# A GLA/attention/MoE decoder on one core: all three parts of the output gate are projected before the head outputs, by step 19

## The chip, the cores and the metric

The kernel runs on one core of a Trainium2 chip. A core has five engines that each work through a queue of instructions of their own and wait for one another by semaphores: TensorE (PE in the profile; its weight loads are PEld), VectorE (DVE), ScalarE (ACT), GpSimd (POOL) and SyncE (SP, which here only issues DMAs). The metric is the device time in microseconds of one execution. Three runs of the kernel before took 1502.73, 1507.63 and 1510.17 us, median 1507.63.

## The reference

Two layers, each a token mixer, a cross-attention into a fixed memory and a mixture of experts, over 512 tokens of width 1024, all in fp32. The change lies in the mixer:

```
h = rms_norm(x, norm_mix[l])
z = h @ w_in[l]          # one projection, split into
(g_q, g_k, g_v, g_lr, g_r, d_q, d_k, d_v, i_q, i_k, i_w, c_u) = split(z)
log_a = log_sigmoid(g_lr @ gla_wa2 + gla_ba) / 16
o_gla = gla_chunked(g_q, g_k, g_v, log_a)        # 4 heads of 48 x 96, with a decaying state
o_gla = rms_norm(o_gla, gla_onorm) * silu(g_r)   # g_r: the output gates, 384 wide
o_dsa = dsa_attention(...)                       # 6 heads, each query keeps its top 128 keys
o_conv = conformer_conv(c_u, ...)                # GLU, 31 causal taps, layer norm, silu
x = x + concat(o_gla, o_dsa, o_conv) @ w_out[l]
x = x + memory_cross_attention(...)
x = x + hierarchical_moe(...)                    # 16 experts, top 1 group, top 2 experts
```

## The kernel before

Each layer has a mixer block, a cross-attention block and an expert block. In the mixer block the columns of w_in come in nine chunks, and each chunk is projected in jobs (the list JOBS): one job fills one bank of PSUM (ps0 and ps1 in turn) by eight pieces, one for each 128 rows of w_in. A job may begin only when ScalarE has copied out the job before the last (the semaphore proj_out). Behind the first jobs (indexer, queries, keys, values) come 24 attention steps: six heads for each of four tiles of 128 queries. Step n handles head n % 6 of tile n // 6, and the width of its work grows with the tile from 128 to 512 keys.

In step n TensorE issues, in this order: the turning of the exponentials of step n by matmuls with a diagonal of inverse sums (L850, "turn n", into the one bank ps6); in even steps the logits of steps n+2 and n+3 (L841) and the values of steps n-2 and n-1 (L862); then the filling work of that step. The filling work is the jobs that attention doesn't need: ca, cg (convolution), gq, gk, gv (the gated linear attention, GLA), kt (keys turned, L742), upd (state parts, three jobs, L750), gr (output gates, three jobs gr0, gr1, gr2 of 128 gate columns each, L728) and o (the outputs of the four GLA heads, L763 and L765). One product of the seven levels of the GLA's decay (L790) goes into each of steps 12 to 18, after the first two pieces of filling. In step 22 comes the sum for the convolution's mean (L899), which needs all taps.

ScalarE in step n: the exponential of step n+1 (L1040); then the copies out of PSUM of all jobs whose last piece stood in step n-1 (L958, for the states L951, for head outputs L939 and behind each but the first a square, L943); only then the copy of turn n out of ps6 (L1059), for which turn n+1 on TensorE waits. VectorE masks (L1205), takes inverses of sums (L1210), merges the level products (L1255), and does the convolution's 62 taps (L1222) spread over steps 5 to 21. GpSimd adds biases, makes the inverse diagonals (L1365), and in the step before STATES clears the buffer of the states (L1390), for which it waits for kt. SyncE loads parts of w_out once the last gv job is done (L664) and once the last o job is done (L666, L667), then mem (L669).

Which job's pieces stand in which step is worked out when the program is built. Each kind of piece has a cost in LENGTH, attention(n) a cost for each step, and for three phases of steps (0 to 3, 4 to 8, 9 to LAST_FILLED - 1) the cost of the phase's jobs and steps divided by the number of steps is its pace. A step takes pieces from the list until its sum reaches the pace; o jobs may not come before step FIRST_O. Steps in which a job ends set other work: STATES (where VectorE adds up the states) is the step after that in which the last upd ends, and the taps are spread by VectorE's estimated load around it. The lines are:

```
LENGTH = dict(ca=0.7, cg=0.7, gq=0.87, gk=0.87, gr=0.87, gv=0.65, kt=0.6, upd=0.7, o=1.5)
GATES, GATED, LAST_FILLED, FIRST_O = 4, 9, 23, 20
```

Of the kernel before, what the change touches and what calls it, by code (L numbers as in the profile page):

```python
# [24 lines left out]
P = 128  # L25
# [3 lines left out]
GH, GK, GV, RANK = 4, 48, 96, 16  # L29
# [99 lines left out]
def program(nc, A, out):  # L129
    ctx = ExitStack()  # L130
    with ctx:
# [8 lines left out]
        def view(t, off, *shape, rows=P):  # L140
            n = int(np.prod(shape))
            ap = t[0:rows, off:off + n]
            names = "abcd"[:len(shape)]
            if len(shape) > 1:
                ap = ap.rearrange(f"p ({' '.join(names)}) -> p {' '.join(names)}",
                                  **{names[i]: shape[i] for i in range(1, len(shape))})
            return ap
# [266 lines left out]
        for l in range(L):  # L414
# [14 lines left out]
            gv = view(arena, up + 3072, NT, GH * GV)  # L429
            gr = view(arena, up + 4608, GC, S)  # L430
# [57 lines left out]
            JOBS = [(0, 0, ID + RANK + IH, "T", "ik", 0)]  # L488
# [6 lines left out]
            JOBS += [(7, 0, GH * GV, "tok", "gv", i) for i in range(NT)]  # L495
            JOBS += [(None, 0, P, "kt", "kt", i) for i in range(2)]
            JOBS += [(8, 0, P, "T", "gr", 0)] + [(None, 0, P, "upd", "upd", c) for c in range(3)]
            JOBS += [(8, P, P, "T", "gr", 1)] + [(None, 0, GV, "o", "o", h) for h in range(2)]
            JOBS += [(8, 2 * P, P, "T", "gr", 2)] + [(None, 0, GV, "o", "o", h) for h in range(2, GH)]
            NJ = len(JOBS)  # L500

            def k_of(chunk):
# [6 lines left out]
            def done(name):  # L509
# [6 lines left out]
                        kt=lambda i: kdecT[:, :, i, :])  # L516
            AFTER_IDX = done("iq")
            STEPS = [(i, h) for i in range(NT) for h in range(AH)]
            NS = len(STEPS)
# [5 lines left out]


            LENGTH = dict(ca=0.7, cg=0.7, gq=0.87, gk=0.87, gr=0.87, gv=0.65, kt=0.6, upd=0.7, o=1.5)
            GATES, GATED, LAST_FILLED, FIRST_O = 4, 9, 23, 20

            def attention(n):  # L530

                i, h = STEPS[n]
                return 0.3 * (i + 1) + (0.9 if 11 <= n < NLEV + 13 else 0.0)

            def filler(names, steps):

                return sum(LENGTH[JOBS[n][4]] for n, c in parts if JOBS[n][4] in names) + sum(attention(n) for n in steps)

            parts, pace = [], 0.0
            for n in range(BEFORE_STEPS, NJ):  # L540
                for c in range(KD if JOBS[n][0] is not None else 1):
                    parts.append((n, c))
            phases = ((("ca", "cg"), range(GATES)), (("gq", "gk"), range(GATES, GATED)),
                      (("gv", "kt", "gr", "upd", "o"), range(GATED, LAST_FILLED)))
            paces = [filler(names, steps) / len(steps) for names, steps in phases]
            work_of, left, spent = [], list(parts), 0.0
            for n in range(NS):
                pace += paces[(n >= GATES) + (n >= GATED)]
                spent += attention(n)
                mine = []  # L550
                while left and (spent < pace or n == NS - 1) and not (JOBS[left[0][0]][4] == "o" and n < FIRST_O):
                    mine.append(left.pop(0))
                    spent += LENGTH[JOBS[mine[-1][0]][4]]
                work_of.append(mine)
# [1892 lines left out]
```

How the kernel before makes its waits and increments, by code:

```python
            def do(ins, mark=None, wait=True):  # L243
                s = sN[mark] if mark else own
                count[s] = count.get(s, 0) + 1
                ins.then_inc(s, 1)
                if wait:
                    eng.wait_ge(s, count[s])
# [6 lines left out]
        def inverse_roots(act, do, banks, n, summed, mark, rows=P, outs=None):  # L255
            for m, bank in enumerate(banks):
                act.wait_ge(sN[summed], m + 1)
                do(nc.scalar.activation(ps[bank][0:rows, :], ps[bank][0:rows, :], ACT.Ln, bias=epst[0:rows, :], scale=1.0 / n))
            for m, bank in enumerate(banks):
                out = outs[m][0:rows, :] if outs else ps[bank][0:rows, :]
                do(nc.scalar.activation(out, ps[bank][0:rows, :], ACT.Exp, scale=-0.5), mark, wait=False)
# [101 lines left out]
        def add_rows(dve, l, k, t):  # L364
            xt = x[:, t, :]
            if k == LAST:
                dve.wait_ge(sN["hot_out"], t + 1)
                dve.wait_ge(s_add, summed(l, HIGH, t))
                rows, g = psw[:, 512 * LAST_BANK(t):512 * LAST_BANK(t) + D], gates[:, t, 1:2]
            else:
                dve.wait_ge(s_yg[NT * k + t], 16 * (l + 1))
                if k == HIGH:
                    dve.wait_ge(s_add, summed(l, LOW, t))
                rows, g = ya[k][t], early[:, t:t + 1] if k == HIGH else gates[:, t, 0:1]
            nc.vector.scalar_tensor_tensor(xt, rows, g, xt, ALU.mult, ALU.add).then_inc(s_add, 1)
```

## Time and profile before

| | |
|---|---|
| runs | 1502.73, 1507.63, 1510.17 us, median 1507.63 |
| profiled execution | 1509.55 us, span 1507.7 us, mean granted TensorE clock 0.979 |
| TensorE busy | 1431.0 us, 95% |
| VectorE busy | 1152.7 us, 76% |
| ScalarE busy | 887.7 us, 59% |
| GpSimd busy | 595.7 us, 40% |
| chain that ended last | PE 46%, DVE 25%, DMA 15%, issue 7%, ACT 5% |
| HBM | 287.76 MB read, 29.50 MB written, 210 GB/s over the span |

Busy time is what an engine computes, without waits. The chain that ended last is followed back from the last instruction, at each step to what released it, and says by engine where the end was decided. The attention steps of layer 0 run from about 127 to 284 us, those of layer 1 from about 870 to 1028 us. In a row of the timeline stand the start and the length in us, the engine, the line, the operation, what it writes and reads, how many instructions were merged, and in square brackets the idle time before the first of them and what ended it. The length of the last matmul is printed up to its modelled end, so the next group can start a little before it is over. One matmul in the program is one or more instructions in the trace (a 512-wide fp32 product is two).

### The profile page before, as it was taken

Reading aid. Unit: us, or ns where it says so; the run is one execution under the profiler, and the core shown is the slowest. Engines: PE = TensorE matmul, PEld = TensorE weight load, DVE = VectorE, ACT = ScalarE, POOL = GpSimd, SP = SyncE. Lnnn points to the kernel's source line nnn. Section 1 sums busy time; section 2 is a strip of 40 time slices with the busy share of each in tenths; the row PEclk is TensorE's granted clock in tenths of the full one; section 3 lists DMA queues with packets and bytes.
Section 4 is the critical chain, followed back from the end, with each engine's and each line's share of the span. In section 5 each row is a group of like instructions: output and inputs, shape, how many; then the busy total and the mean of one; then the engine's idle time right before and its main releaser. Section 6 shows DMA issues by size and latency. Waiting matters only on the chain.

```text
span 1507.7 us, 20546 instructions
## 1 busy us (share of the span) xinstructions
PE 1431.0 (95%) x6830; PEld 1052.0 (70%) x6830; DVE 1152.7 (76%) x1658; ACT 887.7 (59%) x1300; POOL 595.7 (40%) x288
## 2 busy tenths in 40 slices
PE   7999999999999999999799999999989899999995
PEld 4678566567577888877556865665766788887773
DVE  5696887334489999999757958873335899999996
ACT  5733344643558878888485522348345488887880
POOL 2333364060005665554542425521400066655544
PEclk9999999999999999999899999999998899999998
DMA  6333601312149999999651421105041599999995
GB/s 228 95 84 70 222 10 47 140 59 98 70 162 340 399 399 399 398 399 399 216 185 42 112 81 71 57 1 198 1 167 42 183 362 398 398 398 398 398 388 181
DMA packets 151485, 312.75 MB, mean 207 GB/s; under 512 B 33158, under 2 KB 46380, under 8 KB 151228
## 3 DMA queue, kind: packets, MB, share of 16 engines
q1 hardware_dynamic: 140300, 271.39, 49.8%
q0 software_dynamic: 6624, 24.12, 4.3%
q10 hardware_dynamic: 4496, 16.40, 2.7%
q8 instruction: 37, 0.61, 0.2%
q14 instruction: 28, 0.23, 0.0%
HBM read 287.76 MB, written 29.50 MB: 210 GB/s over the span
## 4 chain that ended last, share of the span: by engine, by line
PE 46%; DVE 25%; DMA 15%; issue 7%; ACT 5%; POOL 1%; DVEq 1%; POOLq 0%; SPq 0%; ACTq 0%
PE ps L710 13%; DMA arena<-in_w_down 11%; DVE rest_w_down L1436 8%; PE ps L728 7%; PE ps L1518 4%; DVE rest_w_up L1436 4%; PE ps L1540 3%; DVE rest_w_gate L1436 2%; DVE xg_rest L1449 2%; PE ps L817 2%; PE ps L1636 2%; ACT head_w_down L1431 2%; PE ps L731 2%; DMA arena<-in_w_gate 1%; PE ps L850 1%
## 5 line engine op out<-in xcount | busy, mean ns | idle before, releaser
L2112 POOL TENSOR_TENSOR rest_w_down<-arena,head_w_down 128x2048 fp32r<-128x2048 f32 x30 | 193.4, 6448 | 189.4 <-ACT head_w_down L1431 189.4
L1436 DVE TENSOR_TENSOR rest_w_down<-arena,head_w_down 128x2048 fp32r<-128x2048 f32 x30 | 153.5, 5116 | 12.0 <-ACT head_w_down L1431 11.9
L1436 DVE TENSOR_TENSOR rest_w_gate<-arena,head_w_gate 128x2048 fp32r<-128x2048 f32 x64 | 145.8, 2279 | 0.1
L1436 DVE TENSOR_TENSOR rest_w_up<-arena,head_w_up 128x2048 fp32r<-128x2048 f32 x64 | 143.5, 2281 | 0.1
L1431 ACT ACTIVATE head_w_down<-arena 128x2048 fp32r<-128x2048 f32 x60 | 115.2, 1926 | 39.1 <-DMA arena<-in_w_down 38.9
L1431 ACT ACTIVATE head_w_gate<-arena 128x2048 fp32r<-128x2048 f32 x60 | 114.4, 1919 | 36.1 <-DMA arena<-in_w_gate 35.5
L1431 ACT ACTIVATE head_w_up<-arena 128x2048 fp32r<-128x2048 f32 x64 | 122.0, 1940 | 10.5 <-DMA arena<-in_w_up 10.4
L1420 PE MATMUL ps<-head_w_gate,xg_head 128*128 128x512 f32 x256 | 104.8, 409 | 2.5 <-DVE xg_rest L1449 1.9
L728 PE MATMUL ps<-hT,arena 128*128 128x512 f32 x224 | 104.3, 602 | 2.6 <-ACT arena L951 2.6
L1410 PE MATMUL ps<-head_w_down,he_head 128*128 128x512 f32 x240 | 99.2, 413 | 5.8 <-DVE rest_w_down L1436 2.9
L1422 PE MATMUL ps<-head_w_gate,xg_rest 128*128 128x512 f32 x256 | 101.0, 395 | 0.0
L1421 PE MATMUL ps<-rest_w_gate,xg_head 128*128 128x512 f32 x256 | 101.0, 395 | 0.0
L1420 PE MATMUL ps<-head_w_up,xg_head 128*128 128x512 f32 x256 | 99.8, 390 | 0.0
L1422 PE MATMUL ps<-head_w_up,xg_rest 128*128 128x512 f32 x256 | 99.7, 390 | 0.0
L1421 PE MATMUL ps<-rest_w_up,xg_head 128*128 128x512 f32 x256 | 99.6, 389 | 0.0
L1222 DVE SCALAR_TENSOR_TENSOR mixr<-arena,cf,mixr 128x512 f32<-128x512 f32 x120 | 94.8, 790 | 3.2
L2059 POOL DMA_INDIRECT xg<-hrows,slot_tok x2 | 4.9, 2437 | 229.5 <-DVE slot_tok L2030 229.5
L1411 PE MATMUL ps<-rest_w_down,he_head 128*128 128x512 f32 x240 | 93.9, 391 | 0.0
L1412 PE MATMUL ps<-head_w_down,he_rest 128*128 128x512 f32 x240 | 93.9, 391 | 0.0
L710 PE MATMUL ps<-hT_head,w_rest 128*128 128x512 f32 x224 | 89.8, 401 | 0.0
L2105 POOL DMA_INDIRECT xg<-hrows,idx x28 | 76.4, 2727 | 21.0 <-POOL idx L2118 21.0
L1443 ACT ACTIVATE xg_head<-ps,cf 128x128 fp32r<-128x128 f32 x256 | 69.2, 378 | 25.2 <-PE ps L1712 15.8
(381 smaller groups left out, 3519.2 us busy)
## 6 DMA issues: line engine op xcount, KB each, us to landing
arena<-in_w_gate SPq DMA_DIRECT2D x64, 1024.0 KB, 9.9
arena<-in_w_up SPq DMA_DIRECT2D x64, 1024.0 KB, 11.5
arena<-in_w_down SPq DMA_DIRECT2D x64, 1024.0 KB, 10.7
arena<-in_w_in SPq DMA_DIRECT2D x10, 1536.0 KB, 6.7
yrows<-yb ACTq DMA_DIRECT2D x30, 512.0 KB, 6.2
arena<-in_w_in SPq DMA_DIRECT2D x4, 2048.0 KB, 8.7
x<-in_x SPq DMA_DIRECT2D x8, 512.0 KB, 13.9
arena<-in_w_in SPq DMA_DIRECT2D x16, 256.0 KB, 4.9
```

What stands on the lines that cost most here:

```text
L710: last = nc.tensor.matmul(o, lhs, rhs, start=(c == 0 and a == 0), stop=(c == KD - 1 and a == 2))
L728: last = nc.tensor.matmul(ps[n % 2][0:width, :], w[:, c, col:col + width], hT[:, c, :], start=(c == 0), stop=(c == KD - 1))
L1222: do(nc.vector.scalar_tensor_tensor(o, cin[:, i, j:j + S], convw[:, i, j:j + 1], o, ALU.mult, ALU.add))
L1410: nc.tensor.matmul(out, ah, bh, start=(c == 0), stop=False)
L1411: nc.tensor.matmul(out, ah, bl, start=False, stop=False)
L1412: last = nc.tensor.matmul(out, al, bh, start=False, stop=(c == n - 1))
L1420: nc.tensor.matmul(ps[q][:, :], xh[:, c, :], wh[q][:, c, :], start=(c == 0), stop=False)
L1421: nc.tensor.matmul(ps[q][:, :], xh[:, c, :], wl[q][:, c, :], start=False, stop=False)
L1422: last = nc.tensor.matmul(ps[q][:, :], xl[:, c, :], wh[q][:, c, :], start=False, stop=(c == KD - 1))
L1431: nc.scalar.activation(wh[q][:, part(q, j), :], raw[q][:, part(q, j), :], ACT.Copy).then_inc(s_head[q], 1)
L1436: nc.vector.tensor_tensor(wl[q][:, c, :], raw[q][:, c, :], wh[q][:, c, :].bitcast(F32), ALU.subtract).then_inc(s_split[q], 1)
L2112: nc.gpsimd.tensor_tensor(wl[2][:, c, :], raw[2][:, c, :], wh[2][:, c, :].bitcast(F32), ALU.subtract)\
```

## The change

The list of jobs now has gr1 and gr2 together, ahead of all four head outputs. Phase three is paced over steps 9 to 19 and counts no o jobs. The head outputs have a first step each: 20 for o0 and o1, 22 for o2 and o3.

```
--- before.py
+++ after.py
@@ -495,8 +495,7 @@
             JOBS += [(7, 0, GH * GV, "tok", "gv", i) for i in range(NT)]
             JOBS += [(None, 0, P, "kt", "kt", i) for i in range(2)]
             JOBS += [(8, 0, P, "T", "gr", 0)] + [(None, 0, P, "upd", "upd", c) for c in range(3)]
-            JOBS += [(8, P, P, "T", "gr", 1)] + [(None, 0, GV, "o", "o", h) for h in range(2)]
-            JOBS += [(8, 2 * P, P, "T", "gr", 2)] + [(None, 0, GV, "o", "o", h) for h in range(2, GH)]
+            JOBS += [(8, P * i, P, "T", "gr", i) for i in (1, 2)] + [(None, 0, GV, "o", "o", h) for h in range(GH)]
             NJ = len(JOBS)
 
             def k_of(chunk):
@@ -525,7 +524,7 @@
 
 
             LENGTH = dict(ca=0.7, cg=0.7, gq=0.87, gk=0.87, gr=0.87, gv=0.65, kt=0.6, upd=0.7, o=1.5)
-            GATES, GATED, LAST_FILLED, FIRST_O = 4, 9, 23, 20
+            GATES, GATED, LAST_FILLED, FIRST_O = 4, 9, 20, (20, 20, 22, 22)
 
             def attention(n):
 
@@ -541,14 +540,14 @@
                 for c in range(KD if JOBS[n][0] is not None else 1):
                     parts.append((n, c))
             phases = ((("ca", "cg"), range(GATES)), (("gq", "gk"), range(GATES, GATED)),
-                      (("gv", "kt", "gr", "upd", "o"), range(GATED, LAST_FILLED)))
+                      (("gv", "kt", "gr", "upd"), range(GATED, LAST_FILLED)))
             paces = [filler(names, steps) / len(steps) for names, steps in phases]
             work_of, left, spent = [], list(parts), 0.0
             for n in range(NS):
                 pace += paces[(n >= GATES) + (n >= GATED)]
                 spent += attention(n)
                 mine = []
-                while left and (spent < pace or n == NS - 1) and not (JOBS[left[0][0]][4] == "o" and n < FIRST_O):
+                while left and (spent < pace or n == NS - 1) and not (JOBS[left[0][0]][4] == "o" and n < FIRST_O[JOBS[left[0][0]][5]]):
                     mine.append(left.pop(0))
                     spent += LENGTH[JOBS[mine[-1][0]][4]]
                 work_of.append(mine)
```

By the planner's own figures the pace of phase three goes from 5.16 to 5.70 a step. Where the pieces of filling stand:

| step | before | now |
|---|---|---|
| 10 | gv1 x7 | gv1 x8 |
| 11 | gv1, gv2 x4 | gv2 x7 |
| 12 | gv2 x4, gv3 | gv2, gv3 x5 |
| 13 | gv3 x6 | gv3 x3, kt0, kt1, gr0 |
| 14 | gv3, kt0, kt1, gr0 x2 | gr0 x4 |
| 15 | gr0 x3 | gr0 x3, upd0, upd1 |
| 16 | gr0 x3, upd0 | upd2, gr1 x4 |
| 17 | upd1, upd2, gr1 x3 | gr1 x4 |
| 18 | gr1 x3 | gr2 x4 |
| 19 | gr1 x2 | gr2 x4 |
| 20 | o0, o1, gr2 x3 | o0, o1 |
| 21 | gr2 x4 | none |
| 22 | gr2, o2, o3 | o2, o3 |

STATES goes from step 18 to 17, and with it GpSimd's clearing from step 17 to 16. Of VectorE's taps, step 17 has 0 instead of 3 and step 18 has 6 instead of 3; the others stay.

The order of TensorE's instructions, first from the values of step 16 on (L862 values, L728 gr, L790 level product, L750 upd, L850 turn). Before:

```order
L862 MATMUL ps<-scratch 64x128 x6
L728 MATMUL ps<-hT,arena 128x512 x2
L790 MATMUL ps<-mixg 128x64 x16
L728 MATMUL ps<-hT,arena 128x512
L750 MATMUL ps<-arena 128x192 x2
L850 MATMUL ps<-arena,scratch 128x128 x3
L750 MATMUL ps<-arena 128x192 x4
L790 MATMUL ps<-mixg 128x64 x16
L728 MATMUL ps<-hT,arena 128x512 x3
```

Now, from turn 15 on; a line number of this kernel is one less than before (L727 gr, L789 level product, L749 upd, L849 turn, L840 logits, L861 values):

```order
L849 MATMUL ps<-arena,scratch 128x128 x3
L727 MATMUL ps<-hT,arena 128x512 x2
L789 MATMUL ps<-rs 128x64 x16
L727 MATMUL ps<-hT,arena 128x512
L749 MATMUL ps<-arena 128x192 x4
L849 MATMUL ps<-arena,scratch 128x128 x3
L840 MATMUL ps<-scratch 128x512 x2
L861 MATMUL ps<-scratch 64x128 x6
L749 MATMUL ps<-arena 128x192 x2
L727 MATMUL ps<-hT,arena 128x512
```

Before, upd1 and upd2 (the x4) are followed by a level product and then by gr1's first pieces; now upd0 and upd1 (the x4) close step 15, and turn 16, its logits and values and upd2 stand before gr1.

The second place is the end of step 20 up to step 22, from the last products of o1. Before:

```order
L763 MATMUL ps<-arena 96x128
L765 MATMUL ps<-arena 96x128
L728 MATMUL ps<-hT,arena 128x512 x3
L850 MATMUL ps<-arena,scratch 128x128 x4
L728 MATMUL ps<-hT,arena 128x512 x4
L850 MATMUL ps<-arena,scratch 128x128 x4
L862 MATMUL ps<-scratch 64x128 x8
L728 MATMUL ps<-hT,arena 128x512
L763 MATMUL ps<-arena 96x128 x2
```

Now, from the same products:

```order
L764 MATMUL ps<-arena 96x128
L762 MATMUL ps<-arena 96x128
L764 MATMUL ps<-arena 96x128
L849 MATMUL ps<-arena,scratch 128x128 x8
L861 MATMUL ps<-scratch 64x128 x8
L762 MATMUL ps<-arena 96x128 x2
```

The seven pieces of gr2 between o1 and turn 22 are gone, and turn 21 and turn 22 are printed as one group of eight.

## Rows read from the trace of the kernel before

**Rows 1.** Busy time by window, the attention steps of layer 0 and of layer 1.
```profile
core 0: us, PE busy (x) PEld busy (x) DVE busy (x) ACT busy (x) POOL busy (x), PEclk, DMA share, GB/s
126.80:284.00 157.20, 152.52 (x876) 100.40 (x875) 113.98 (x203) 60.54 (x137) 60.31 (x60) 0.99 0.24 85
870.40:1027.60 157.20, 152.54 (x876) 100.43 (x875) 114.02 (x203) 60.53 (x137) 60.00 (x60) 0.99 0.16 58
```

**Rows 2.** Waits of TensorE (line waiting, what it waited for: us, times, longest), 150 to 284 us.
```profile
PE ps L728 <- ACT arena L951: 1.3, 1, 1.3
PE ps L862 <- ACT scratch L1059: 0.9, 1, 0.9
PE ps L790 <- ACT arena L1051: 0.2, 1, 0.2
PE ps L742 <- ACT arena L958: 0.2, 1, 0.2
```

**Rows 3.** Timeline of TensorE, steps 16 to 18 (start, us, engine, line).
```profile
233.39 0.83 PE L850 MATMUL ps<-arena,scratch 128*128 128x128 f32 x6
...
236.02 1.98 PE L728 MATMUL ps<-hT,arena 128*128 128x512 f32 x4
...
242.15 1.47 PE L750 MATMUL ps<-arena 128*128 128x192 f32 x8
...
246.85 2.84 PE L728 MATMUL ps<-hT,arena 128*128 128x512 f32 x6 [1.30 <-ACT arena L951]
```

**Rows 4.** Timeline of TensorE, steps 20 to 22.
```profile
260.11 1.05 PE L850 MATMUL ps<-arena,scratch 128*128 128x128 f32 x8
...
266.32 2.74 PE L728 MATMUL ps<-hT,arena 128*128 128x512 f32 x6
268.89 1.05 PE L850 MATMUL ps<-arena,scratch 128*128 128x128 f32 x8
269.78 3.60 PE L728 MATMUL ps<-hT,arena 128*128 128x512 f32 x8
...
279.25 1.88 PE L899 MATMUL ps<-mixr,ones 128*128 128x512 f32 x4
```

**Rows 5.** Timeline of ScalarE, around step 21.
```profile
264.55 0.72 ACT L1040 ACTIVATE scratch<-scratch,small 128x512 f32<-128x512 f32 x1 [0.61 <-DVE small L1205]
...
266.52 1.79 ACT L939 ACTIVATE mixg<-ps 32x512 f32<-32x512 f32 x3 [0.68 <-PE ps L765]
268.33 0.63 ACT L943 ACTIVATE rs<-mixg 128x512 f32<-128x512 f32 x1
269.98 0.60 ACT L1059 ACTIVATE scratch<-ps 128x512 f32<-128x512 f32 x1 [1.02 <-PE ps L850]
```

**Rows 6.** Page, costliest groups: the convolution taps.
```profile
L1222 DVE SCALAR_TENSOR_TENSOR mixr<-arena,cf,mixr 128x512 f32<-128x512 f32 x120 | 94.8, 790 | 3.2
```

**Rows 7.** Timeline of VectorE: behind the last tap of layer 0.
```profile
269.36 0.06 DVE L1308 MEMSET small<- 128x1 f32 x1
```

**Rows 8.** Timeline of TensorE: the first matmuls behind four gaps.
```profile
128.87 0.49 PE L850 MATMUL ps<-arena,scratch 128*128 128x128 f32 x2 [2.04 <-POOL arena L1365]
...
373.91 2.34 PE L1606 MATMUL ps<-arena 64*128 64x256 f32 x14 [2.49 <-DVE arena L1895]
...
1117.55 1.78 PE L1606 MATMUL ps<-arena 64*128 64x256 f32 x14 [2.49 <-DVE arena L1895]
...
1479.12 0.47 PE L2177 MATMUL ps<-head_w_gate,he_head 128*128 128x512 f32 x1 [2.11 <-DVE he_rest L2321]
```

**Rows 9.** Busy time and granted clock (PEclk) by window, behind those gaps.
```profile
129.20:132.60 3.40, 3.40 (x12) 2.61 (x11) 3.23 (x10) 0.77 (x3) 1.21 (x3) 0.51 0.70 263
375.00:378.40 3.40, 3.40 (x14) 2.31 (x11) 2.79 (x4) 1.78 (x8) 0.00 (x0) 0.50 1.06 393
1117.60:1121.00 3.40, 3.40 (x23) 2.78 (x24) 2.13 (x3) 0.73 (x3) 0.00 (x0) 1.00 1.05 387
1479.20:1482.60 3.40, 3.40 (x15) 2.81 (x16) 0.81 (x1) 0.00 (x0) 0.71 (x1) 1.00 0.38 154
```

More of the change, by code:

```diff
@@ L497, in program @@
             JOBS += [(8, 0, P, "T", "gr", 0)] + [(None, 0, P, "upd", "upd", c) for c in range(3)]
-            JOBS += [(8, P, P, "T", "gr", 1)] + [(None, 0, GV, "o", "o", h) for h in range(2)]
-            JOBS += [(8, 2 * P, P, "T", "gr", 2)] + [(None, 0, GV, "o", "o", h) for h in range(2, GH)]
+            JOBS += [(8, P * i, P, "T", "gr", i) for i in (1, 2)] + [(None, 0, GV, "o", "o", h) for h in range(GH)]
             NJ = len(JOBS)
@@ L527, in program @@
             LENGTH = dict(ca=0.7, cg=0.7, gq=0.87, gk=0.87, gr=0.87, gv=0.65, kt=0.6, upd=0.7, o=1.5)
-            GATES, GATED, LAST_FILLED, FIRST_O = 4, 9, 23, 20
+            GATES, GATED, LAST_FILLED, FIRST_O = 4, 9, 20, (20, 20, 22, 22)
             def attention(n):
@@ L543, in program @@
             phases = ((("ca", "cg"), range(GATES)), (("gq", "gk"), range(GATES, GATED)),
-                      (("gv", "kt", "gr", "upd", "o"), range(GATED, LAST_FILLED)))
+                      (("gv", "kt", "gr", "upd"), range(GATED, LAST_FILLED)))
             paces = [filler(names, steps) / len(steps) for names, steps in phases]
@@ L550, in program @@
                 mine = []
-                while left and (spent < pace or n == NS - 1) and not (JOBS[left[0][0]][4] == "o" and n < FIRST_O):
+                while left and (spent < pace or n == NS - 1) and not (JOBS[left[0][0]][4] == "o" and n < FIRST_O[JOBS[left[0][0]][5]]):
                     mine.append(left.pop(0))
```

## The prediction

> **What bounds the kernel now.** The page comes first. TensorE is busy 95% of the span, and in the chain that ended last it has the largest share, so the first question is whether it ever stands still where the change works. The change is inside the 24 attention steps of each layer. The busy times by window show this stretch twice: 152.52 us of TensorE work in 157.20 us in layer 0, 152.54 in the same length in layer 1 [rows 1]. The two layers are the same here to 0.02 us, so I work out layer 0 and double it. Next come the waits of TensorE in the steps of layer 0 that carry projections of the gate and later chunks: 1.3 us for the states' copies, 0.9 us at the very end, 0.2 us twice [rows 2]. That is 2.6 us. All other engines have idle time in this stretch that nobody waits for. TensorE's work is therefore the bound, the change keeps that work (the same instructions in another order), and no order can save more than 2.6 us a layer. What it can do is make new idle time on TensorE. So the sum is one of waits, not of work.
>
> **The change part by part.** *What is moved.* The third part of gr (gr2, eight pieces of two matmuls) is now projected in steps 18 and 19, not in 20 to 22. By the row of eight matmuls that take 3.44 us to the next start (269.78, printed as 3.60 with its tail), a piece costs 0.86 us, eight 6.9 us [rows 4]. gv, kt, upd and gr1 move forward to make room. The jobs are only reordered: 0 us of work on TensorE. Turn 20, at 260.11 before, comes up to 6.9 us later, and everything behind it has 6.9 us less to do.
>
> *The states' wait that goes.* Before, upd0 stood in step 16 and upd1 and upd2 in step 17. They run from 242.15, one level product follows, and gr1's first piece starts only at 246.85, having idled 1.30 us until ScalarE had copied the state parts [rows 3]. It waits for the copy of upd1, which ScalarE takes up only behind the exponential of step 18. In the new order upd0 and upd1 close step 15, and turn, logits, values and upd2 of step 16 lie between upd1 and the first piece of gr1. Turn, logits and values of step 16 run from 233.39 to 236.02, 2.6 us, and one upd is half of the 1.47 us printed for two [rows 3]: 3.3 us in all, against the copies of gr0, upd0 and upd1, which at 0.60 us or a little over (a 512-wide copy, [rows 5]) are 2 us. I take the whole 1.30 us: -1.3.
>
> *Waits it adds before step 20.* upd1 now stands behind gr0's last piece with only upd0 between, and needs gr0's copy out of its bank. The copy takes 0.60 us and upd0 0.7 us of issue; with the matmul's tail (0.16 us between printed length and next start in most of [rows 4]) and two semaphores some 0.2 us are left: +0.2. Bounds are 0 and 0.8, the latter if ScalarE has just begun an exponential of 0.72 us [rows 5]. kt0 and kt1 now stand together; before, a level product of 2 us stood between them and 0.19 us of wait were left [rows 2]. Now kt1 waits for gv3's copy with only kt0, three transposes, as its cover: +0.2, with the same bounds for the same reason. GpSimd clears the states' buffer one step earlier and waits for kt1 there; what stands behind it on GpSimd is the bias of step 17 and the inverse of step 15, and the cleared buffer is needed some 10 us later: 0. Three convolution taps of 0.79 us [rows 6] move from step 17 to 18; all taps end at 269.36 [rows 7] and their mean is formed at 279.25 [rows 4], ten us later: 0. SyncE's loads of w_out and mem hang on the last head output, which moves by the sum below and no more.
>
> *The wait it makes in step 21.* This is the largest term. After head outputs o0 and o1 TensorE does turn 21, and turn 22 must wait until ScalarE has copied the result of turn 21 out of the one bank they share. ScalarE has queued, ahead of that copy, the three copies of o1 and a square. Before: o1's issue ends at 266.32, its copies run 266.52 to 268.31, the square to 268.96, and the copy of turn 21 comes at 269.98 [rows 4, 5]. TensorE never noticed, since three pieces of gr2 stood between o1 and turn 21 and four between turn 21 and turn 22. With no gr2 left, call the end of o1's issue E. Turn 21 runs E to E+0.89. ScalarE is free at E+2.64 (268.96 less 266.32), copies for 0.60, and turn 22 starts at E+3.28. TensorE idles 3.28 less 0.89: +2.4. Bounds: 2.0, if the square overlaps more than shown, and 3.2, if the exponential of step 22 is late and pushes o0's copy into o1's. VectorE and GpSimd are not later than this: once turn 20 is over, the mask of step 22, its exponential (0.72), three taps (0.79 each) and the inverse follow within an estimated 6 us by these lengths, and turn 22 stands more than 9 us behind turn 20.
>
> *Behind it.* Turn 22, values, o2, o3, the mean's product and turn 23 follow as before; the 0.9 us at the end (values 22, behind o3's copies) stays, as does the 0.2 us of the last level product [rows 2]: 0.
>
> Sum of waits: -1.3 +0.2 +0.2 +2.4 = +1.5 us a layer, +3.0 in all. By the bounds it is -1.3 +2.0 = +0.7 to -1.3 +0.8 +0.8 +3.2 = +3.5 a layer.
>
> *The clock.* TensorE idled 2.0 to 2.5 us at one go in six places of the span. Four stand in [rows 8]: 2.04 us before 128.87, 2.49 before 373.91 and again before 1117.55, 2.11 before 1479.12. In the 3.4 us just behind them (from 375.00 in the second case, where the level changed) the granted clock was 0.51, 0.50, 1.00 and 1.00 [rows 9]. The other two repeat the first, one at the same place of layer 1 and one before the last expert block of layer 0, with most of the stretch at half. So it is 1.2 GHz in four of six cases, 2.4 GHz in two. The new wait of 2.4 us is of this size, and none of the old ones in these steps is. What follows it is TensorE work without cover, so 3.4 us at half rate cost 1.7 us. With four in six it falls in one layer or in both: +1.7 or +3.4.
>
> The Trainium skill bears on this: "TensorE: Matmul & The Clock Gate", section "Why this matters for your kernels", says that throughput holds as long as no idle gap between bursts of matmuls is longer than one that is somewhat above this wait. By that rule the clock would stay up and the sum be +3.0. Four of the six rows just named speak against it and two for it, so it has its own case below.
>
> The sum is made against the profiled execution: span 1507.7, 1509.55 us with what lies around it. That is 1.9 us above the median of the runs shown, 1507.63, and inside their spread. Forecast: waits +3.0 and one fall of the clock +1.7, together +4.7, from 1507.63: 1512.3 us.
>
> **The rivals.**
> *The clock stays up.* The gaps of layer 1 before 1117.55 and 1479.12 show it can [rows 8, 9]. Then +3.0: 1510.6. (It is what the page of the Trainium skill named above would give.)
> *It falls in both layers.* Four of six gaps speak for it. Then +6.4: 1514.0.
> *Slower beyond doubt: a longer stretch at 1.2 GHz.* One mechanism, in step 21 of both layers: the wait behind o1's copies comes out near its upper bound 3.2 us (+0.8 a layer) and the clock stays down until the second wait, 0.9 us at values 22 some 9 us later, that is for about twice 3.4 us, costing 3.4 us a layer. Then 2 x (1.5 + 0.8 + 3.4) = +11.4: 1519.0. It decides from where the idle time in step 21 exceeds those six gaps. For it: the two waits lie close together. Against it: 0.9 us is far below the gaps that cost the clock.
> *Faster: the new wait is covered.* If the copy of turn 21 gets in before o1's last copies, or TensorE's own order leaves work between the two turns, only -1.3 +0.4 stay: -0.9 a layer, -1.8: 1505.8. Against it: ScalarE runs its queue in order, and before it, too, the copies of o1 came ahead of that of turn 21 [rows 5].
> *The change does not do what it says.* A planner sets the steps; the instruction order shows the third part of gr done before turn 20 and nothing of it after, so only the price can be nought: if the new wait merely replaces the old one, 1507.6. The lower bound +0.7 a layer is near it.
> *VectorE becomes the bound.* From the mask of step 19 it has 23 taps, 18 us [rows 6], and four masks and inverses, some 22 us together, and may start only after turn 17, near 248. It would end near 270, when TensorE is at turn 21. Ten us of room speak against it; I give it no time of its own.
>
> **How the numbers follow.** What a measurement of this kernel can tell from no change is about 0.5%, 7.5 us. Chances: one fall 0.35, clock up 0.22, both falls 0.22, longer low stretch 0.09, waits merely exchanged 0.07, faster 0.05. The first three all lie at +3 to +6.4, within 0.5%; with the spread of the medians (the three runs differ by 7.4 us) a third of the both-falls case and a tenth of the one-fall case may read as slower, which with the long stretch gives 0.20. Of the faster case a half would read as such: 0.03. Same 0.77. The range runs from the faster case, 1505, to just short of the long stretch, 1518.
>
> **What would show it.** Right: on TensorE in step 21 of both layers an idle gap of 2.4 us before the matmuls of turn 22, ended by ScalarE's copy of turn 21; the 1.3 us before gr1 gone; small waits at upd1 and kt1; the granted clock near 0.5 just behind the gap in one layer or both; the end of the steps 1.5 us later per layer plus 1.7 per fall. Wrong: turn 22 starting right behind turn 21; the steps shorter than before; or the end of the taps later than the last head output.

## The result

The changed kernel took 1512.55 us (median of nine runs, 1510.38 to 1516.24), the kernel before 1507.63 us beside it. One of the nine executions of the kernel before took 4994.01 us and is not in the ratio; the other eight have a median of 1506.82. The ratio is 1.0038, 95% interval 1.0024 to 1.0052: some 0.4% or 5.7 us slower. The interval leaves out 1, and the size is inside the 0.5% that the prediction called no change. In a second set of runs on another occasion it was 1.0048 (1.0034 to 1.0062).

The waits of TensorE in the attention steps of layer 0, in the columns of [rows 2]; all lines of the changed kernel are one lower than before:

```profile
PE ps L849 <- ACT scratch L1058: 2.4, 1, 2.4
PE ps L861 <- ACT scratch L1058: 0.9, 1, 0.9
PE ps L741 <- ACT arena L957: 0.4, 1, 0.4
PE ps L789 <- ACT arena L1050: 0.3, 1, 0.3
```

The 1.3 us behind the states' copies are gone and 2.4 us for ScalarE's copy of a turn (L1058) are new. The 0.9 us at the end are the same, the wait at the turned keys is 0.4 instead of 0.2 (L741), and the one at the last level product, 0.3 instead of 0.2 in this print, is 0.25 us in the timelines of both kernels. The timeline of TensorE shows where, with the same place of layer 1 last; it answers [rows 3, 4]:

```profile
219.16 0.55 PE L741 MATMUL ps<-cf,arena 128*128 128x128 f32 x3 [0.41 <-ACT arena L957]
...
234.02 1.77 PE L749 MATMUL ps<-arena 128*128 128x192 f32 x8
...
239.01 1.02 PE L727 MATMUL ps<-hT,arena 128*128 128x512 f32 x2
...
264.95 1.13 PE L840 MATMUL ps<-scratch 64*128 64x512 f32 x4
...
270.17 1.06 PE L849 MATMUL ps<-arena,scratch 128*128 128x128 f32 x8
...
273.58 1.44 PE L849 MATMUL ps<-arena,scratch 128*128 128x128 f32 x8 [2.36 <-ACT scratch L1058]
...
276.86 1.06 PE L762 MATMUL ps<-arena 128*96 128x128 f32 x4
...
280.37 1.88 PE L898 MATMUL ps<-mixr,ones 128*128 128x512 f32 x4
...
284.04 1.09 PE L861 MATMUL ps<-scratch 128*64 128x128 f32 x16 [0.90 <-ACT scratch L1058]
...
1021.29 1.61 PE L849 MATMUL ps<-arena,scratch 128*128 128x128 f32 x8 [2.36 <-ACT scratch L1058]
```

Turn 21 starts at 270.17, right behind o1, and turn 22 only at 273.58, having idled 2.36 us; in layer 1 the same. Turn 22 is printed with 1.44 us where turn 21 has 1.06 with the same work. ScalarE at that place, answering [rows 5]:

```profile
268.84 0.59 ACT L938 ACTIVATE mixg<-ps 96x512 f32<-96x512 f32 x1 [0.35 <-PE ps L764]
270.37 1.79 ACT L938 ACTIVATE mixg<-ps 32x512 f32<-32x512 f32 x3 [0.94 <-PE ps L764]
272.19 0.63 ACT L942 ACTIVATE rs<-mixg 128x512 f32<-128x512 f32 x1
272.84 0.60 ACT L1058 ACTIVATE scratch<-ps 128x512 f32<-128x512 f32 x1
273.34 0.72 ACT L1039 ACTIVATE scratch<-scratch,small 128x512 f32<-128x512 f32 x1
```

o0's copy, three copies of o1, the square, the copy of turn 21, the exponential, one behind another. The square ends at 272.82, 2.65 us after 270.17 where o1's issue ends; 2.64 was worked out. The copy of turn 21 ends at 273.44, and turn 22 starts 0.14 us later. The busy times by window, the first two from turn 6 (the first one 256 keys wide) to the first head-sum product behind the steps, (L909 now, L910 before) in layers 0 and 1, then in each layer the 3.4 us that begin 0.7 and 0.5 us after the start of turn 22:

```profile
core 0: us, PE busy (x) PEld busy (x) DVE busy (x) ACT busy (x) POOL busy (x), PEclk, DMA share, GB/s
166.24:285.07 118.83, 114.87 (x720) 74.14 (x718) 86.84 (x136) 48.47 (x107) 49.12 (x44) 0.99 0.17 58
913.98:1032.77 118.79, 114.86 (x719) 74.13 (x717) 86.86 (x136) 48.46 (x107) 48.82 (x44) 0.99 0.08 28
274.30:277.70 3.40, 3.40 (x24) 2.85 (x23) 0.10 (x1) 0.60 (x1) 0.60 (x1) 0.50 0.02 5
1021.80:1025.20 3.40, 3.40 (x24) 2.85 (x23) 0.16 (x1) 0.35 (x2) 0.60 (x1) 0.50 0.00 0
```

The same two stretches of the kernel before:

```profile
core 0: us, PE busy (x) PEld busy (x) DVE busy (x) ACT busy (x) POOL busy (x), PEclk, DMA share, GB/s
168.60:283.94 115.34, 112.70 (x720) 72.92 (x718) 86.49 (x136) 48.62 (x107) 49.00 (x44) 1.00 0.17 60
912.24:1027.56 115.32, 112.69 (x719) 72.92 (x717) 86.52 (x136) 48.61 (x107) 48.69 (x44) 1.00 0.08 29
```

The stretch is 118.83 instead of 115.34 us, 3.5 us longer in each layer, and the granted clock is 0.50, which is 1.2 GHz, behind both new waits. Twice 3.5 is 7.0 us, yet this profiled execution took only 1510.38 us against 1509.55. The rest of the program was 6 us shorter in that one execution, for a reason that no run here shows: it began the stretch 2.4 us earlier, and from the end of layer 1's steps to the end it took 475.7 us instead of 480.1, with work that the change leaves alone. A profile taken again (first experiment) has 118.80 and 118.84 us in the stretches and needs 477.0 us for that last part. The stretches of a kernel repeat to 0.2 us between layers and between executions, the total does not, so I read the stretches first and the timed runs as a check on them.

### The profile page after: what moved, and what is told of

Read it like the earlier page. It is cut to its first block, busy times and chain, and to the rows that moved or that the text cites. A ratio compares the mean times of both kernels' runs of the same rounds, so it can differ in the third digit from the quotient of the medians.

```text
span 1508.5 us, 20544 instructions
## 1 busy us (share of the span) xinstructions
PE 1432.8 (95%) x6830; PEld 1051.6 (70%) x6830; DVE 1151.9 (76%) x1658; ACT 888.1 (59%) x1300; POOL 596.9 (40%) x288
## 4 chain that ended last, share of the span: by engine, by line
PE 48%; DVE 23%; DMA 15%; issue 6%; ACT 6%; DVEq 1%; POOL 0%; SPq 0%; ACTq 0%; POOLq 0%
PE ps L709 13%; DMA arena<-in_w_down 12%; DVE rest_w_down L1435 8%; PE ps L727 7%; PE ps L1517 4%; DVE rest_w_up L1435 3%; PE ps L1539 3%; DVE rest_w_gate L1435 2%; ACT head_w_down L1430 2%; PE ps L816 2%; DVE xg_rest L1448 2%; PE ps L1635 2%; PE ps L730 2%; PE ps L849 1%; DMA arena<-in_w_gate 1%
## 5 line engine op out<-in xcount | busy, mean ns | idle before, releaser
L727 PE MATMUL ps<-hT,arena 128*128 128x512 f32 x224 | 104.3, 602 | 0.0
```

The source lines that it names most:

```text
L727: last = nc.tensor.matmul(ps[n % 2][0:width, :], w[:, c, col:col + width], hT[:, c, :], start=(c == 0), stop=(c == KD - 1))
```

## The experiments

Theory A says that the loss is made in step 21, by the wait for ScalarE and the low clock behind it. Theory B, its rival, says that it comes from the longer steps 10 to 19. E is the time at which TensorE has issued the last product of o1. All ratios are to the kernel before, run beside them. "Stretch" is the time from turn 6 to the first head-sum product, layer 0; before it is 115.34 us and in the change 118.83.

**The change again.** No edit.

> The changed kernel itself, beside the three below on the same chip. Both theories: about 1.004 of the kernel before (+5 us). Theory A (the loss sits in step 21: +1.5 us of waits a layer and 1.7 us a layer of 1.2 GHz behind the new wait): +4.7 to +6.4 us; in its trace turn 22 waits 2.4 us in both layers. Theory B (the loss comes from the longer steps 10 to 19, step 21 is beside the point): the same total, but the time from the load of the head masks to step 20 grows by more than the 6.9 us that were moved there.

Measured 1513.44 us, 1.0048 (1.0034 to 1.0062); both stretches 118.8, both new waits 2.35 us, both followed by 3.4 us at 1.2 GHz. Theory B's sign is not there: from turn 6 (166.24) to turn 20 (263.97 at its start) it is 97.73 us, before (168.60 to 260.11) 91.51. (Starts from the first profile.) That is 6.2 us more for 6.9 us of moved work, so the forward part gained 0.7 us.

**The copy of turn 21 ahead of those of o1.** On ScalarE:

```
+                    late = ended_in(n - 1)[-1:] if n == 21 else []
                     for job in ended_in(n - 1) if n else ():
-                        evacuate(job)
+                        if job not in late:
+                            evacuate(job)
                     turned(n)
+                    for job in late:
+                        evacuate(job)
```

> The changed kernel, but in step 21 ScalarE copies turn 21 out before it copies o1 (nothing else moves). Theory A: turn 21 is copied at E+1.1 to E+1.7, so TensorE idles about 0.85 us before turn 22 instead of 2.4, and the granted clock stays up behind it: 1.5 + 1.7 us a layer less than the changed kernel, 6.4 us, or 1.000 to 0.998 of the kernel before. Theory B: no different from the changed kernel, 1.004.

Measured 1505.22 us, 0.9993 (0.9983 to 1.0003): the loss is gone, to within the interval, by four instructions of ScalarE in another order, with TensorE's order untouched. Turn 21 and turn 22 on TensorE, and the two stretches:

```profile
270.14 1.06 PE L849 MATMUL ps<-arena,scratch 128*128 128x128 f32 x8
...
271.97 1.13 PE L849 MATMUL ps<-arena,scratch 128*128 128x128 f32 x8 [0.78 <-ACT scratch L1058]
```

```profile
core 0: us, PE busy (x) PEld busy (x) DVE busy (x) ACT busy (x) POOL busy (x), PEclk, DMA share, GB/s
166.22:281.88 115.66, 113.30 (x719) 72.82 (x718) 86.86 (x136) 48.45 (x107) 49.08 (x44) 1.00 0.17 60
910.95:1026.62 115.67, 113.30 (x719) 72.82 (x717) 86.87 (x136) 48.44 (x107) 48.77 (x44) 1.00 0.08 29
```

The wait is 0.78 us (0.85 expected), there is no low clock, and the stretch is 115.66, 3.17 us below the change against 3.2 expected. It is still 0.3 us above before: turn 21 to turn 22 takes 1.83 us where turn 21 alone takes 0.89, and those 0.94 us are more than the 0.7 that the forward part gained. Steps 10 to 19 are as in the change, so this settles A against B.

**Two products in the wait.** On TensorE, `if n == 22: idle_products(2)` ahead of turn(n).

> The changed kernel with two products that nothing reads (512 wide, about 1.7 us) on TensorE between turn 21 and turn 22, which fill the wait without shortening it. Theory A with the clock as told: turn 22 starts no earlier, about 0.65 us of idle time are left, the granted clock is 1.0 behind it in both layers, and the time is 2 x 1.7 = 3.4 us below the changed kernel, about 1.002 of before. Rival (the clock costs nothing, since what follows is bound by ScalarE's copies): the clock goes up and the time stays at 1.004.

Measured 1511.61 us, 1.0026 (1.0014 to 1.0038). TensorE from turn 21 to turn 22, then the busy time in the stretch of layer 0 and in the 3.4 us behind turn 22's start:

```profile
272.94 1.06 PE L849 MATMUL ps<-arena,scratch 128*128 128x128 f32 x8
273.83 1.89 PE L401 MATMUL ps<-ones 128*128 128x512 f32 x4
276.35 1.13 PE L849 MATMUL ps<-arena,scratch 128*128 128x128 f32 x8 [0.63 <-ACT scratch L1060]
```

```profile
core 0: us, PE busy (x) PEld busy (x) DVE busy (x) ACT busy (x) POOL busy (x), PEclk, DMA share, GB/s
169.01:286.26 117.25, 115.03 (x724) 73.44 (x722) 86.90 (x136) 48.43 (x107) 49.10 (x44) 1.00 0.17 59
276.40:279.80 3.40, 3.40 (x36) 3.11 (x37) 0.16 (x1) 1.10 (x3) 0.60 (x1) 1.00 0.03 5
```

0.63 us of idle time are left, the clock is 1.00, and the stretch 117.25 instead of 118.83. Turn 22 starts 3.41 us after turn 21 here (272.94 to 276.35) as in the change (270.17 to 273.58), so the wait costs the same in both, and all of the 1.58 us lies behind turn 22: from its start to the first head-sum product it is 9.91 us instead of 11.49. The low clock alone is worth 1.58 us a layer, 3.2 in all (3.4 expected). The timed runs agree but would not show it by themselves: the ratios differ by 0.0022, 3.3 us, the medians by 1.8, and the intervals of this kernel (to 1.0038) and of the change (from 1.0034) overlap.

What is left above 115.34 is 1.91 us a layer of waits, where +1.5 was forecast. From start to start, turn 21 to turn 22 takes 3.41 us where turn 21 alone takes 0.89, so the wait costs 2.52 where 2.4 was forecast; up to turn 20 the gain was 0.66 where 0.9 was forecast (-1.3 +0.2 +0.2); the other 0.05 lie behind turn 22. Of the smaller gain, 0.1 is the wait at upd1 and the rest is not traced to one place.

**LAST_FILLED 21.** `GATES, GATED, LAST_FILLED, FIRST_O = 4, 9, 21, (20, 20, 22, 22)`.

> The changed list of jobs with LAST_FILLED 21 instead of 20: the pace is lower, gr2 ends in step 20, o0 and o1 stand in step 21, o2 and o3 in 22. All parts of the gates are still ahead of the head outputs. Theory A: ScalarE's copies of o0 and o1 now stand ahead of the copy of turn 22, behind which TensorE has values, o2, o3 and the mean, so the 2.4 us wait and the fall of the clock are gone and the 1.3 us before gr1 stay gone: 1.0 to 1.4 us a layer below the kernel before, 0.998. Theory B (it is the forward move that costs): between before and the changed kernel, 1.002 to 1.004.

Measured 1504.53 us, 0.9987 (0.9976 to 0.9999), the lowest median of all. TensorE behind step 21, and the stretches:

```profile
273.59 1.06 PE L849 MATMUL ps<-arena,scratch 128*128 128x128 f32 x8
...
282.40 1.09 PE L861 MATMUL ps<-scratch 128*64 128x128 f32 x16 [0.89 <-ACT scratch L1058]
```

```profile
core 0: us, PE busy (x) PEld busy (x) DVE busy (x) ACT busy (x) POOL busy (x), PEclk, DMA share, GB/s
169.26:283.43 114.17, 112.45 (x720) 72.98 (x718) 87.25 (x136) 48.38 (x107) 48.50 (x44) 1.00 0.18 61
913.18:1027.33 114.15, 112.43 (x719) 72.97 (x717) 87.20 (x136) 48.38 (x107) 48.19 (x44) 1.00 0.09 29
```

o0 and o1 now stand in step 21, and turn 22 (273.59) follows them with no wait, since the copies of o0 and o1 are in ScalarE's queue ahead of the copy of turn 22, not of turn 21. One wait of 0.58 us, before gr0, is new. The stretch is 114.17: 1.17 us a layer below before, within the 1.0 to 1.4 expected, and 4.66 below the change. The same gates ahead of the same head outputs gain or lose by one step's place.

**The forward move with gr2 kept as cover.** The kernel before with `LAST_FILLED` 22 instead of 23. The planner then also puts o2 and o3 into step 21, behind the last piece of gr2, and leaves steps 19 and 22 empty.

> The kernel before with LAST_FILLED 22 instead of 23 and nothing else: gv, kt, gr0, upd and gr1 are moved forward nearly as in the change (gr1 ends in step 18, the upd jobs stand together in step 16), but gr2 stays behind o0 and o1, seven pieces in step 20 and one in 21. Theory A: the forward move alone gains the 1.3 us before gr1 and pays some small waits of TensorE; seven pieces of gr2 cover ScalarE's copies of o1, so no wait of over 1 us appears in steps 20 to 22 and the clock stays up: 0.5 to 0.9 us a layer less than before, 0.999. Theory B (longer steps 10 to 19 are the cost): above before, 1.002 or more.

Measured 1506.91 us, 0.9995 (0.9984 to 1.0007), stretch 115.27: no loss, as A says, but a gain of 0.07 us instead of 0.5 to 0.9. The waits of layer 0 that are printed, but for one of 0.25:

```profile
259.73 1.13 PE L850 MATMUL ps<-arena,scratch 128*128 128x128 f32 x8 [0.78 <-ACT scratch L1059]
...
266.70 6.28 PE L728 MATMUL ps<-hT,arena 128*128 128x512 f32 x14 [0.53 <-ACT mixg L939]
...
283.30 1.09 PE L862 MATMUL ps<-scratch 128*64 128x128 f32 x16 [0.69 <-ACT scratch L1059]
```

The 1.30 us before gr1 are gone, but 0.78 us before turn 20 (step 19 has no filling left in this plan) and 0.53 before gr2 (it needs o0's copy) are new. I had left the first of them out of the sum. Here, too, the work moved forward brings no loss near that of the change, which speaks against Theory B (1.002 or more).

**Three more copies ahead of the copy of turn 21.** On ScalarE, in the kernel before and in the change:

```
                         evacuate(job)
+                    if n == 21:
+                        for _ in range(3):
+                            do(nc.scalar.activation(ps[7], ones[:, 0:1].to_broadcast([P, 512]), ACT.Copy))
                     turned(n)
```

> The kernel before with three more copies of 0.6 us (ones into a free bank of PSUM, read by nobody) on ScalarE in step 21, ahead of the copy of turn 21: ScalarE's queue there is about 1.9 us longer. Theory A: with four pieces of gr2 (3.4 us) between turn 21 and turn 22 they are hidden, since the copy of turn 21 ended at 270.58 and turn 22 began at 273.22: 0 to 0.1 us, 1.000. Theory that any work added to ScalarE in these steps costs its length: +3.8 us, 1.0025.

> The changed kernel with the same three copies at the same place. Theory A: nothing hides them, the wait before turn 22 grows from 2.4 to about 4.3 us in both layers, and the time by 1.9 us a layer: 3.8 us above the changed kernel, 1.007 of before; the clock falls behind it as before, perhaps for longer. Theory B (step 21 is beside the point): no more than the changed kernel, 1.0045.

In the kernel before: 1506.79 us, 0.9998 (0.9986 to 1.0010), stretch 115.33. In the change: 1519.39 us, 1.0078 (1.0064 to 1.0092), stretch 121.98. ScalarE in the kernel before, with the three copies and the copy of turn 21:

```profile
268.61 1.85 ACT L1083 ACTIVATE ps<-ones 128x512 f32<-128x512 f32 x3
270.48 0.60 ACT L1059 ACTIVATE scratch<-ps 128x512 f32<-128x512 f32 x1
```

and turn 22 in the change with them, with the granted clock of the 6.8 us from 278.1 on:

```profile
278.62 2.05 PE L849 MATMUL ps<-arena,scratch 128*128 128x128 f32 x8 [4.12 <-ACT scratch L1058]
```

```profile
core 0: us, PE busy (x) PEld busy (x) DVE busy (x) ACT busy (x) POOL busy (x), PEclk, DMA share, GB/s
278.10:284.90 6.80, 6.28 (x35) 5.75 (x36) 0.16 (x1) 1.67 (x4) 0.60 (x1) 0.50 0.01 2
```

In the first the copies run under gr2's pieces and cost nothing: they start in time that ScalarE had spent idle, and the copy of turn 21 still ends (at 271.08) 1.9 us before turn 22, where it had ended 2.6 us before it [rows 4, 5]. In the second the wait grows from 2.36 to 4.12 us (4.3 expected). The stretch grows by 3.15 us, of which 1.76 are wait. The other 1.4 are the clock: from turn 22 to the first head-sum product it is 12.89 us instead of 11.49, since the clock was low for 6.8 us from 278.1 instead of for 3.4 us. It fell 0.5 us before turn 22 started, while TensorE still stood still. A longer fall was left open in the expectation ("perhaps for longer") and not priced, so its +3.8 us in all is short of the 6.2 us by which the two stretches grow. The ratios, 1.0078 against 1.0048, differ by 4.5 us.

## Why the prediction was right

The forecast was 1512.3 us, the measured median 1512.55. The mechanism was right, and that the two medians agree to 0.3 us is in part luck. The forecast added 4.7 us, the two stretches grew by 7.0 together (3.8 of waits where 3.0 were forecast, 3.2 of clock where 1.7 were), and the ratios stand for 5.7 and 7.2 us. By its steps:

- *The states' wait, -1.3.* Right: no wait before the first piece of gr1 (239.01). Before it was 1.30 [rows 3].
- *Small waits, +0.2 and +0.2.* The keys' wait rose from 0.19 (printed as 0.2 in [rows 2]) to 0.41, as said. The upd1 wait is not printed as idle time, since it lies inside a group: eight instructions of upd are printed with 1.77 us at 234.02, and with 1.47 in [rows 3]. That is 0.3. Right in kind, a little small.
- *The wait in step 21, +2.4.* Right: 2.36 us are printed in both layers, by the mechanism told, shown by the reordered copies and by the longer ones. In the prediction's own reckoning it was 0.13 more: turn 22 started at E+3.41, where it said E+3.28. Its terms, E+2.64 and a copy of 0.60, give 3.24; it names nothing for the other 0.04. Measured were 2.65 to the end of the square, 0.62 more to the end of the copy, and 0.14 from there to the start of turn 22.
- *Waits behind it, 0.* Right: 0.9 us at values 22 in both kernels. The taps ended at 271.8, nine us before their mean at 280.37.
- *The clock.* The size was right (1.58 us a fall, 1.7 forecast), the count was the step that missed. The forecast took one fall as likeliest and the rival two. Both profiles of the change show two of two, and the reordered and the filled kernel none. By its own rows "both layers" gave 1514.0, +6.4, and the stretches, 7.0 us longer together, stand nearer to that case than to the forecast one (+4.7). So do the timed runs taken together: 5.7 and 6.9 us above before by their medians.
- *What the Trainium skill says of idle gaps* ("TensorE: Matmul & The Clock Gate", "Why this matters for your kernels") would have kept the clock up here; four of four new waits of 2.4 us in the two profiles say otherwise, and the measurement decides. The waits of 0.8 us left the clock up.
- *Rivals.* The wait being covered, and VectorE as the bound, did not happen. The longer low stretch did not happen in the change, but is what three more copies brought.

## What to carry to other kernels

Work that an engine finishes early was perhaps the cover of another engine's queue. Before moving filling work away, look at what the other engine has queued ahead of the result that the first one needs next: here 2.6 us of copies and a square stood there unnoticed under seven pieces of gr2, 6.0 us of products. When such a wait appears, put the awaited copy first in the queue or shift the block by one step. Here the two gave back 3.2 and 4.7 us a layer for a printed wait of 2.4 us, since TensorE also ran 3.4 us at half rate behind each such wait. Filling the wait with products that nothing reads gave back only the 1.6 us of the clock.

## What the runs showed of the hardware that was not expected

The new wait of 2.36 us (2.35 in the second profile) was followed by 3.4 us at 1.2 GHz in both layers of both profiles of the change (four of four), with the fall between the start of turn 22 and 0.8 us after it. The wait of 4.12 us had 6.8 us of it in both layers, beginning while TensorE still stood still. Waits of 0.63 and 0.78 us in the same place had none behind them. The length of the wait alone does not decide: in the kernel before, two of six gaps of 2.0 to 2.5 us left the clock up [rows 8, 9], and of two shorter gaps there, one of 1.85 us was followed by the low clock and one of 1.88 us was not.

```profile
387.12 1.09 PE L1616 MATMUL ps<-cf,mixg 128*128 128x128 f32 x8 [1.88 <-DVE mixg L1907]
...
456.29 0.50 PE L1420 MATMUL ps<-head_w_gate,xg_head 128*128 128x512 f32 x1 [1.85 <-DVE xg_rest L1449]
```

```profile
core 0: us, PE busy (x) PEld busy (x) DVE busy (x) ACT busy (x) POOL busy (x), PEclk, DMA share, GB/s
387.60:391.00 3.40, 3.40 (x13) 1.78 (x12) 0.69 (x1) 1.25 (x2) 0.00 (x0) 1.00 0.00 0
456.80:460.20 3.40, 3.40 (x9) 2.62 (x9) 3.40 (x4) 3.40 (x5) 0.17 (x1) 0.52 0.99 340
```

What decides between them stays open.
